# Shifting every buffer behind a certain point of on-chip memory by 64 bytes, in a one-core kernel of two transformer-like blocks

## The reference

```
def peer_ffn(h, q_w, subkey1, subkey2, expert_u, expert_v):
    ...
        expert = e1 * PEER_KEYS + e2
        g = jax.nn.softmax(top_s, axis=-1)
        u = jnp.take(expert_u, expert, axis=0)
        act = jax.nn.gelu(jnp.einsum('thkd,td->thk', u, xc).astype(jnp.float32), approximate=False)
        w = (g * act).astype(xc.dtype)
        return jnp.einsum('thk,thkd->td', w, jnp.take(expert_v, expert, axis=0))
```

## Time and profile before

| what | value |
|---|---|
| median of 3 runs | 2524.07 us (2521.89 to 2526.58) |
| the profiled execution, its own time | 2525.84 us |
| its span, first to last instruction | 2524.1 us |
| PE busy | 2453.1 us, 97% of the span, 18,074 products |
| PEld busy | 2275.1 us, 90% |
| DVE / ACT / POOL busy | 73% / 49% / 49% |
| mean granted TensorE clock | 0.982 |
| chain of waits, share of PE | 84% |

### The profile page before, as it was taken

One profiled execution on the slowest core, in us unless ns is written; L12 is line 12 of the kernel. 1 busy time (PEld: TensorE's weight loads), 2 busy tenths in 40 slices (PEclk: granted clock), 3 DMA queues, 4 the chain that ended last, 5 costly groups with the idle time before them and its releaser, 6 DMA issues.

```text
span 2524.1 us, 47109 instructions
## 1 busy us (share of the span) xinstructions
PE 2453.1 (97%) x18074; PEld 2275.1 (90%) x18074; DVE 1831.7 (73%) x3366; ACT 1246.8 (49%) x2150; POOL 1230.0 (49%) x525
## 2 busy tenths in 40 slices
PE   7999999989899999999999999999999999999999
PEld 7999999988899999998888888889999999888887
DVE  6857783668749899987777775563997999555555
ACT  6345543455555544444444454555454444444444
POOL 5547787645679977760000014456997676100000
PEclk9999999989999999999999998999999999999999
DMA  5435787732456655548777763334665454566664
GB/s 172 137 93 184 239 318 254 266 117 83 135 176 193 201 159 155 156 143 280 253 252 258 257 193 100 101 109 151 198 194 174 155 158 153 184 192 192 192 192 142
DMA packets 126063, 457.94 MB, mean 181 GB/s; under 512 B 13984, under 2 KB 15392, under 8 KB 125600
## 3 DMA queue, kind: packets, MB, share of 16 engines
q1 hardware_dynamic: 118512, 425.56, 53.4%
q10 hardware_dynamic: 7344, 29.49, 3.3%
HBM read 453.95 MB, written 1.05 MB: 180 GB/s over the span
## 4 chain that ended last, share of the span: by engine, by line
PE 84%; DVE 9%; issue 3%; ACT 2%; DMA 1%; POOL 1%; SPq 0%; DVEq 0%; POOLq 0%; ACTq 0%
PE mm L1297 28%; PE ms L1337 28%; PE mm L812 17%; PE ms L1318 3%; DVE work L1994 1%; POOL low L1937 1%; DVE hs L1994 1%; PE ms L819 1%; DVE work L1988 1%; PE ms L827 1%; DVE scratch L1994 1%; DVE work L1991 1%; PE mm L981 1%; PE mm L819 1%; DVE mm L1988 0%
## 5 line engine op out<-in xcount | busy, mean ns | idle before, releaser
L1937 POOL TENSOR_TENSOR low<-ring,high 128x1024 fp32r<-128x1024 f32 (+2 forms) x502 | 1216.2, 2437 | 915.3 <-ACT high L1548 758.7
L1802 ACT ACTIVATE high<-ring 128x1024 fp32r<-128x1024 f32 x506 | 535.8, 1059 | 355.6 <-PE ms L1337 324.6
L1297 PE MATMUL mm<-hs,high 128*128 128x256 f32 x4096 | 520.4, 280 | 3.4 <-ACT high L1548 3.4
L1337 PE MATMUL ms<-high,wts 128*128 128x512 f32 x2048 | 510.8, 392 | 0.0
L2573 DVE TENSOR_TENSOR low<-ring,high 128x1024 fp32r<-128x1024 f32 x256 | 313.4, 1225 | 248.3 <-ACT high L1802 248.3
L1297 PEld LDWEIGHTS mm<-hs,high 128*128 128x128 f32 x4096 | 486.8, 188 | 3.8 <-issue 3.8
L1337 PEld LDWEIGHTS ms<-high,wts 128*128 128x128 f32 x2048 | 384.2, 188 | 84.0
L1548 ACT ACTIVATE high<-ring 128x1024 fp32r<-128x1024 f32 (+2 forms) x252 | 258.2, 1030 | 126.5 <-PE mm L812 98.1
L812 PE MATMUL mm<-hs,high 128*128 128x256 f32 x2192 | 286.3, 284 | 7.5 <-DVE parts L1988 3.9
L812 PEld LDWEIGHTS mm<-hs,high 128*128 128x128 f32 x2192 | 268.2, 191 | 12.9 <-ACT high L1548 7.2
L1337 PE MATMUL ms<-low,wts 128*128 128x512 f32 x1024 | 276.1, 391 | 3.0 <-DVE low L2573 3.0
(11 more groups left out here) (342 smaller groups left out, 3070.0 us busy)
## 6 DMA issues: line engine op xcount, KB each, us to landing
ring<-w_peer_experts SPq DMA_DIRECT2D x512, 512.0 KB, 3.9
work<-w_mod ACTq DMA_DIRECT2D x48, 512.0 KB, 5.6
ring<-w_late_mods SPq DMA_DIRECT2D x48, 512.0 KB, 4.5
ring<-w_ffn_up SPq DMA_DIRECT2D x44, 512.0 KB, 5.1
ring<-w_peer_q SPq DMA_DIRECT2D x32, 512.0 KB, 3.7
ring<-w_fox_in SPq DMA_DIRECT2D x32, 512.0 KB, 3.5
ring<-w_lru_in SPq DMA_DIRECT2D x22, 512.0 KB, 3.5
ring<-w_gates SPq DMA_DIRECT2D x16, 512.0 KB, 3.6
```

Source lines behind the costliest of these rows:

```text
L1297: ins_ = pe.matmul(mm[:, s_ % BANKS, 0:T], w_[:, k * P:(k + 1) * P], hs[:, b_, k, :], start=pass_ == 0 and k == 0, stop=pass_ == 2 and k = ...
L1337: ins_ = pe.matmul(ms[:, 2 * c + half, :], wts[:, s_ % 3, b_, c * P:(c + 1) * P], v_[:, half * 512:(half + 1) * 512], start=s_ == 0 and pa ...
L1802: act.activation(high[:, (q0 + i) % CUT, :], ring[:, n_ % RAW, :], ACT.Copy) \
L1937: pool.tensor_tensor(low[0:rows, cut_slot, 0:width], ring[0:rows, raw_slot, 0:width], high[0:rows, cut_slot, 0:width].bitcast(F32), ALU.su ...
```

## The change

More of the change, by code:

```diff
@@ L461, in build @@
         tiny = sb("tiny", [P, 512])
+        sb("to_line", [P, 16])
         with nc.sbuf_tensor("parts", [P, 2 * FFG * T], F32R) as parts_:
```

## The result

The changed kernel took 2570.97 us in the median of 4 runs (2563.6 to 2572.3), against 2525.32 us of the kernel before (2521.89 to 2529.29). The ratio is 1.017, 95% interval 1.0149 to 1.019. The forecast was 2524 us, within 2496 to 2554; the kernel is slower, and slower than the range held for possible.

What follows compares the result with a forecast made beforehand. PE was taken to bound the kernel, busy 2453.1 of 2524.1 us, so only its products' pitch could move the time. All four parts were 0, giving 2524 us against the median, range 2496 to 2554.

Steps and rivals of the forecast that it cites:

- Part 1 of the sum: Hidden and dense products, 256 columns, moving `hs`, `parts` or `raw` against `high` or `low`: taken as 0.
- The bound of that part: Range for each 256-column product: -4.6 ns where the slow rhythm goes, +4.6 ns where it comes.
- the slower rival: Hidden products (L1297) take the slow rhythm: 28 us more, 2552 us, or 2564 us with dense products; chance 0.20.
- Part 2: Value products, 512 columns, stationary `wts`, moving `high` or `low`: taken as 0, bounds 44 us less and 14 us more.
- the forecast rival: Faster rival: the misplaced operand costs the excess pitch of PE's products; 2498 us, or 2464 us in full; chance 0.24.
- small form: Dense products lose the slow rhythm, 12 us, and value products 14 us: 2498 us; about two thirds of 0.24.
- Parts 3 and 4: DVE, ACT and POOL on `work`, `hs` and `wts`, and transfers of 48 tiles into `work`: each taken as 0.
- The argument against it: Eight products on the low part of `raw` already have this placement and cost at most 1.2 ns more.

Runs made afterwards that it cites:

- hs_alone: Kernel before with `hs` moved to a multiple of 128, `wts` moved by 128 bytes in all and `work` left in place: 2583.63 us, 1.022 of before.
- wts_alone: Kernel before with only `wts` moved to a multiple of 128: 2525.52 us, 0.9987 of before.
- The six kernels of the table: Kernel before with `hs` and `wts` at six other pairs of distances from `high`: 2568.26, 2555.84, 2563.76, 2572.79, 2584.88 and 2546.9 us.

## Why the prediction was wrong

- *What bounds the kernel* was right: PE, by its pitch, and only its pitch moved.
- *Part 1 of the sum failed, the 256-column products at 0.* The step was the choice of the nearest rows. The 258-column rows of `raw` were taken for a pair with both operands in phase; but each of their rows begins 8 bytes further, only one in eight has its start where the argument needed it, and the mean over eight hides what a single distance does. The starts of the single products show it: the first eight from 678.64 have pitches of 118, 121, 116, 119, 120, 124, 122 and 119 ns, so two neighbours, 8 bytes apart, differ by up to 5 ns. The float32 products are another form, and they indeed stayed at 3.62 us for 16 in the changed kernel. Neither is a float32r product of 256 columns whose distance stays the same from product to product. The trace before also held the swapped products, the same two buffers with their roles and so their distance changed: 117.0 ns in the mean, against 114.9 for the dense ones with moving `hs`. They were not read; they would not have given 120.0, but they point upward. In place of 0 the term measured +36.3 us for hidden and +19.8 us for dense products.
- *The bound of that part failed too.* The upper end was +4.6 ns, the step between the two rhythms that a row showed. The changed operands have a rhythm of their own, 120.0 ns, 6.7 ns above the fast one. Hidden products were to cost at most 28 us in the slower rival; they cost 36.3. Its top, 2564 us, was left out of the range as a case of 0.08, and even that lies 7 us below the result.
- *Part 2* took 0 for the value products within -44 and +14 us; it was -6.4 us, of the forecast rival's sign but half the size of its small form.
- *Parts 3 and 4* at 0 held: no other engine's busy time grew by more than 2.2 us, and the waits of PE's groups moved by a few us in both directions (0.8 us more before L1338, 2.9 less before the dense products with `hs` and `high`). The tiles into `work` took 4.7 us each after 5.6; in hs_alone and wts_alone, which leave `work` where it was, it is 5.0 and 5.9, so this says nothing of its address.
- *The slower rival* had the place (L1297), the mechanism (the moving operand's phase against the stationary one's) and the sign right, with a chance of 0.20. Two of its parts were off: the phase is not that of a 128-byte line (one of 256 bytes fits), and 0 does not choose between the two known rhythms but makes a third. Its own mark, a pitch of 117.9 ns, did not appear.
- *The argument against it*, the low part of `raw`, was the same misreading as in part 1.

The trace had a sign that was priced too low: the same products on the same buffers ran at 113.3 and 117.9 ns. That does not show that addresses matter, but it shows that something besides the number of columns sets the pitch. Nothing in the trace bounded that from above, for 9,000 products at once, so the range should not have been closed at the value that happened to be seen.

The pitch of one and the same form goes with the distance of its two operands, hidden products from 113.3 to 120.0 ns. The Trainium skill, "SBUF — State Buffer", section "Who interferes with whom", calls PE's two read ports, for the moving operand and for weight loads, independent. These traces do not show what happens at the ports, but a pitch that depends on where the two operands lie to each other is not what independent reads lead one to expect. Its "TensorE: Matmul & The Clock Gate", section "Back-to-back issue gap", gives N/2.4 + 2.5 ns for a product by itself, by which 256 and 512 columns come to 109.2 and 215.8 ns, an estimate; no distance tried reaches either, the best are 113.3 and 226.7.

What stays open: by what mechanism the distance acts, why 192 is best for one form and 0 for the other, and what chooses between the two rhythms at 192. Distances between the steps of 32 bytes were not tried with 256 or 512 columns, nor bfloat16 products with their weights at other distances. The six kernels of the table ran once each.

## What to carry to other kernels

When PE is never idle, read the pitch of its products in the timeline, form by form, and treat two pitches for one form as a warning that more than the number of columns sets it; relative addresses are then worth a try. Rounding buffers to a round number is no rule here: the distance between moving and stationary operand, modulo 256 bytes, is a parameter to be tried for each form, and it was worth 6% of a 256-column and 3% of a 512-column float32r product. Move one buffer at a time, as the good half of such a change can be had without the bad one (2517.5 us against 2525.1 of the kernel before beside it; the changed kernel had 2571.0 against 2525.3).

## What the runs showed of the hardware that was not expected

- The pitch of float32r products depends on the distance of their two operands: 113.3 to 120.0 ns with 256 columns, 226.7 to 234.3 ns with 512, at a granted clock of 1.00. Both operands shifted together by 64 bytes change nothing (543.5 us in both kernels).
- At a distance of 192, 256-column products have two rhythms, 113.3 and 117.8 ns, each kept over hundreds of products; at 0 the undisturbed hidden phases show only 120.0. The slow one in both layers cost 11 us in wts_alone. That may be a part of the scatter of the kernel before, 2517.8 to 2538 us over all its runs, but this is not shown: only one execution of it was traced, and the changed kernel, without the two rhythms, still scatters by 9 us.
- Float32 products in two passes do not answer to it: 3.62 us for 16 with `work` against `ring` at either distance.
